# Writing a weight stream out in full on SyncE and GpSimd, in a kernel bound by TensorE

## The reference

```python
for l in range(DEPTH):                      # first_block
    h = x @ w_in[l]
    ...                                     # four attention groups -> mix
    y = _group_rmsnorm(mix, mix_g[l]) @ w_o[l]
    x = _layernorm(ALPHA * x + y, ln1_g[l], ln1_b[l])
    f = (jax.nn.silu(x @ w_gate[l]) * (x @ w_up[l])) @ w_down[l]
    x = _layernorm(ALPHA * x + f, ln2_g[l], ln2_b[l])
for l in range(DEPTH):                      # second_block
    h = x + 0.5 * swiglu(rms_norm(x, ffn1_norm[l]), ffn1_gate[l], ffn1_up[l], ffn1_down[l])
    z = rms_norm(h, mix_norm[l]) @ w_in[l]
    ...                                     # attention, convolution, RG-LRU
    h = h + jnp.concatenate([y_da, y_sc, y_lru], axis=-1) @ w_out[l]
    x = h + 0.5 * swiglu(rms_norm(h, ffn2_norm[l]), ffn2_gate[l], ffn2_up[l], ffn2_down[l])
return rms_norm(x, final_norm)
```

## Time and profile before

| what | value |
| --- | --- |
| median of 3 runs | 3143.33 us (3143.02 to 3143.93) |
| span of the profiled execution | 3141.2 us |
| time of the profiled execution beyond its span | not given; the median is 2.1 us above the span |
| busy share PE, POOL, DVE, ACT | 99%, 72%, 37%, 23% |
| mean granted TensorE clock | 0.998 |

### The profile page before, as it was taken

How to read it: one execution, slowest core, us unless ns; L and a number is a source line. 1 busy time by engine, 2 the same in 40 slices (tenths; PEclk the granted TensorE clock), 3 DMA queues, 4 the chain that set the end, 5 groups by cost and what they waited for, 6 DMA issues and landing times.

```text
span 3141.2 us, 44673 instructions
## 1 busy us (share of the span) xinstructions
PE 3116.4 (99%) x15518; PEld 2588.2 (82%) x15518; DVE 1147.4 (37%) x1874; ACT 713.8 (23%) x1474; POOL 2259.0 (72%) x3079
## 2 busy tenths in 40 slices
PE   8999999999999999999999999999999999999999
PEld 7879888898798888888887788888888887788887
DVE  5575111275751112632226542212222136542211
ACT  4453110054531100411112321110211022321100
POOL 5347877673468776788777398887888777398884
PEclk9999999999999999999999999999999999999999
DMA  5112322231123222232232132223222232132222
GB/s 185 48 41 86 109 93 95 93 108 42 47 88 104 96 95 90 84 102 98 95 112 92 41 101 95 98 95 100 94 94 100 94 111 88 41 108 94 100 94 68
DMA packets 83017, 284.07 MB, mean 90 GB/s; under 512 B 9531, under 2 KB 15068, under 8 KB 82652
## 3 DMA queue, kind: packets, MB, share of 16 engines
q1 hardware_dynamic: 77484, 273.70, 26.2%
q10 hardware_dynamic: 5424, 8.79, 0.8%
HBM read 278.79 MB, written 3.67 MB: 90 GB/s over the span
## 4 chain that ended last, share of the span: by engine, by line
PE 97%; DVE 2%; ACT 1%; issue 0%; DMA 0%; DVEq 0%; ACTq 0%
PE bank_v L537 21%; PE bank_v L539 20%; PE bank_v L538 20%; PE bank_a L537 9%; PE bank_a L539 9%; PE bank_a L538 9%; PE bank_v L881 1%; PE bank_a L860 1%; PE bank_s L1021 1%; PE bank_s L899 1%; PE bank_v L1036 1%; PE bank_s L591 0%; PE bank_s L1024 0%; PE bank_a L584 0%; PE bank_s L889 0%; PE bank_s L907 0%
## 5 line engine op out<-in xcount | busy, mean ns | idle before, releaser
L511 POOL TENSOR_TENSOR w_lo<-raw,w_hi 128x512 fp32r<-128x512 f32 x1024 | 1414.7, 1382 | 81.8
L508 POOL TENSOR_TENSOR zero<-zero 128x1 f32<-128x1 f32 x1024 | 277.3, 271 | 769.0 <-PE bank_v L539 578.8
L537 PE MATMUL bank_v<-xn_hi,w_hi 128*128 128x512 f32 (+1 forms) x1680 | 640.9, 381 | 8.1 <-DVE xn_lo L1700 8.0
L509 POOL CAST w_hi<-raw 128x512 fp32r<-128x512 f32 x1024 | 639.1, 624 | 0.0
L539 PE MATMUL bank_v<-xn_hi,w_lo 128*128 128x512 f32 (+1 forms) x1680 | 635.0, 378 | 0.0
L538 PE MATMUL bank_v<-xn_lo,w_hi 128*128 128x512 f32 (+1 forms) x1680 | 634.6, 378 | 0.0
L537 PE MATMUL bank_a<-xn_hi,w_hi 128*128 128x512 f32 (+1 forms) x1232 | 469.0, 381 | 2.3 <-ACT work L1248 1.4
L539 PE MATMUL bank_a<-xn_hi,w_lo 128*128 128x512 f32 (+1 forms) x1232 | 466.7, 379 | 0.0
L538 PE MATMUL bank_a<-xn_lo,w_hi 128*128 128x512 f32 (+1 forms) x1232 | 466.6, 379 | 0.0
L537 PE MATMUL bank_v<-h_hi,w_hi 128*128 128x512 f32 (+1 forms) x1122 | 422.9, 377 | 0.0
L538 PE MATMUL bank_v<-h_lo,w_hi 128*128 128x512 f32 (+1 forms) x1122 | 422.4, 376 | 0.0
(11 more groups left out here) (357 smaller groups left out, 3114.5 us busy)
## 6 DMA issues: line engine op xcount, KB each, us to landing
raw<-in_w_stream SPq DMA_DIRECT2D x516, 512.0 KB, 3.3
rope<-in_rope ACTq DMA_DIRECT2D x2, 1024.0 KB, 5.7
da_v<-t_rows ACTq DMA_DIRECT2D x2, 1024.0 KB, 6.5
out<-resid SPq DMA_DIRECT2D x8, 256.0 KB, 2.3
t_rows<-t_row ACTq DMA_DIRECT2D x1, 1536.0 KB, 7.4
resid<-in_x ACTq DMA_DIRECT2D x5, 256.0 KB, 7.2
mla_v<-in_alibi ACTq DMA_DIRECT2D x2, 512.0 KB, 7.5
resid<-in_x SPq DMA_DIRECT2D x3, 256.0 KB, 9.4
```

What stands on the lines that cost most here:

```text
L508: pool.tensor_tensor(zero[:, 1:2], zero[:, 0:1], zero[:, 0:1], ALU.add)
L509: pool.tensor_copy(w_hi[:, u, cut], raw[:, u, cut]).then_inc(*hi_split.done(("unit", u, n)))
L511: ins = pool.tensor_tensor(w_lo[:, u, cut], raw[:, u, cut], w_hi[:, u, cut].bitcast(F32), ALU.subtract)
L537: pe.matmul(out, lhs_hi, rhs_hi, start=first, stop=False)
```

## The change

Both loops are written out in Python over n = 4 to 515: each of the 512 units gets its own instructions, in which the waits compare with constants and the DMA's address is constant. The one-column addition ahead of each half is left out. The order of the loads, casts and subtractions, and what each waits for, stays. The programs of TensorE, VectorE and ScalarE are untouched.

```diff
-            with loop(sp, "stream", UNITS // SLOTS - 1) as i:
-                for u in range(SLOTS):
-                    sp.wait_ge(*w_split.before(("unit", u)))
-                    sp.dma_start(raw[:, u, :], t["w_stream"][i + 1, u]
-                                 ).then_inc(*raw_in[u].done("unit", 16))
+            for n in range(SLOTS, UNITS):
+                u = n % SLOTS
+                sp.wait_ge(*w_split.before(("unit", n)))
+                sp.dma_start(raw[:, u, :], t["w_stream"][n // SLOTS, u]).then_inc(*raw_in[u].done(("unit", n), 16))
...
-            with loop(pool, "stream", UNITS // SLOTS - 1):
-                for u in range(SLOTS):
-                    pool.wait_ge(*raw_in[u].after("unit"))
-
-                    for n, (left, cut) in enumerate(((half_used, slice(0, UNIT // 2)), (w_used, slice(UNIT // 2, UNIT)))):
-                        pool.wait_ge(left.sem, w_split.before(("unit", u))[1])
-                        pool.tensor_tensor(zero[:, 1:2], zero[:, 0:1], zero[:, 0:1], ALU.add)
-                        pool.tensor_copy(w_hi[:, u, cut], raw[:, u, cut]).then_inc(*hi_split.done(("unit", u, n)))
-                        pool.wait_ge(*hi_split.after(("unit", u, n)))
-                        ins = pool.tensor_tensor(w_lo[:, u, cut], raw[:, u, cut], w_hi[:, u, cut].bitcast(F32), ALU.subtract)
-                    ins.then_inc(*w_split.done(("unit", u)))
+            for n in range(SLOTS, UNITS):
+                u = n % SLOTS
+                pool.wait_ge(*raw_in[u].after(("unit", n)))
+                for k, (left, cut) in enumerate(((half_used, slice(0, UNIT // 2)), (w_used, slice(UNIT // 2, UNIT)))):
+                    pool.wait_ge(left.sem, w_split.before(("unit", n))[1])
+                    pool.tensor_copy(w_hi[:, u, cut], raw[:, u, cut]).then_inc(*hi_split.done(("unit", n, k)))
+                    pool.wait_ge(*hi_split.after(("unit", n, k)))
+                    ins = pool.tensor_tensor(w_lo[:, u, cut], raw[:, u, cut], w_hi[:, u, cut].bitcast(F32), ALU.subtract)
+                ins.then_inc(*w_split.done(("unit", n)))
```

## The result

| | before | after |
| --- | --- | --- |
| median (range) | 3143.93 us, 9 runs (3143.02 to 3144.33) | 3152.17 us, 9 runs (3146.81 to 3152.7) |
| ratio of the means, 95% interval | | 1.0023 (1.0014 to 1.0033) |
| profiled execution: span, mean clock | 3141.2 us, 0.998 | 3147.0 us (its time 3148.76), 0.998 |

The changed kernel is slower, by some 8 us in the median, and it has come to spread over 6 us where the kernel before keeps within 1.3. Ten more executions of it had a median of 3149.36 us (3147.71 to 3154.67), so the cost is 6 to 8 us. The forecast of 3143.2 us in 3141.0 to 3146.5 was wrong.

A forecast was written before the change was run, and what follows sets the result against it. TensorE was taken to bound the kernel; additions, waits, SyncE and code each brought 0 and VectorE's shifts -0.1 us on 3141.2 us, which with the median's 2.1 us offset gave 3143.2 us, range 3141.0 to 3146.5 us.

The forecast's parts named there:

- What bounds the kernel: Whole span: TensorE, busy 3116.4 of 3141.2 us, sets the time; none of its waits names GpSimd or a load.
- The additions go: GpSimd, 1024 one-column additions: removing them saves 133 us of GpSimd's occupancy (bounds 0 and 277) and 0 on TensorE.
- the 4.7 us of waits on VectorE: TensorE's waits: up to 4.7 us end on VectorE and could shrink; rival put at 3141.0 us, chance 0.08.
- The terms of GpSimd: GpSimd's busy time falls 133 us to about 2126, the cast's mean rises towards 700 ns, idle time grows as much.
- the excess of 79.7 us: GpSimd's additions: their time above the median, spent held; said to pass to the cast and not be saved.
- the sign's 2090 to 2150: GpSimd (POOL): busy time in us that would show the forecast right.
- The 2230 us given for an unrelieved GpSimd: GpSimd: rival that the start-up of 0.13 us passes to the cast; busy some 2230 us, time 3143.3 us, chance 0.04.
- Register waits, SyncE, code length: GpSimd's and SyncE's streams: constant waits save 0 to 6 us of GpSimd, none of TensorE; SyncE and longer code 0.
- As many may go away as come: VectorE's steps ahead of waiting matmuls: argument against new collisions, that those gained and lost may balance.
- VectorE's late steps collide anew: VectorE ahead of waiting matmuls: earlier casts hold a step by 1.09 us; three net collisions give 3146.6 us, chance 0.07.
- The rival on late refills: First projections and halved norms: instruction fetches delay GpSimd's refills, 2.6 us a hit; 3146 to 3151 us, chance 0.05.
- The clock: TensorE: two half-clock stretches of about 3.4 us, full elsewhere; one more or fewer is worth 1.7 us, within the range.

The follow-up runs named there:

- the kernels with the shortest middle waits (6.1, 6.9 and 7.2 us): On the changed kernel: no subtraction at the edges, 3139.49 us; additions and halved subtractions at the edges, 3143.94 us; every subtraction halved, 3143.82 us.

## Why the prediction was wrong

*What bounds the kernel*: right as far as it went. TensorE is busy for 99% (3118.1 us, 1.7 more than before, where at most 1 was expected), and no wait of it ends on GpSimd, before or after.

*The additions go; "on TensorE it is worth 0, because no wait of TensorE is ended by GpSimd"*: this is the step that failed, and what covers it was taken to be GpSimd's own slack. The waits name the last releaser only. GpSimd reaches TensorE through VectorE: a subtraction that has the port makes VectorE's next two-input step 1.1 us longer, and in the halved norms and the attention VectorE's steps release matmuls with nothing to spare. The prediction had both halves, the stretched step of the earlier trace rows and the 4.7 us of waits on VectorE, but its sum gave them -0.1 us, and it gave new collisions a chance of 0.07. It never asked which engine comes first at the port, with and without the additions. At 270 us of the trace before, the distance of 0.10 us could have been read. In place of the 0 the runs show 4.4 us more of TensorE's waits, and a median 8.2 us longer; with the additions back it is 3142.57 us.

*The terms of GpSimd*: the fall of its busy time was put at 133 us and is 161. The cast's mean was to rise to 700 ns and rose to 658, and its waiting for TensorE grew to 935.8 us, where 850 to 900 were expected. Of the excess of 79.7 us, 34.7 came to the cast and 19.4 to the subtraction; and the rest is gone from GpSimd. That POOL's 2097.7 us lie within the sign's 2090 to 2150 is no proof of the terms. The 2230 us given for an unrelieved GpSimd follow from no row.

*Register waits, SyncE, code length*: right as far as can be measured. With the additions kept, all three together give a ratio of 0.9987 to 1.0005, and SyncE alone 0.9992 to 1.0010. The instruction traffic grew by 24 packets and 0.2 MB.

*"As many may go away as come"*: wrong. The collisions that came (9 held steps against 5, and three longer attention steps) outweigh those that went. In the norms they repeat, since the cycles of the two engines keep step. The rival "VectorE's late steps collide anew" named the mechanism and the price of 1.09 us, and its 3146.6 us for three net collisions is near the fastest executions. Its sign, middle waits above 12 us, came true too (12.4, though 2.7 of them end on ScalarE). It had a chance of 0.07 only. The rival on late refills fell: no run with the subtraction whole made TensorE wait more than 0.5 us for GpSimd.

*The clock*: 1.7 us for one stretch was right. "At full elsewhere" was not: the matmuls up to 12.6 us run at half the clock too. Taking the clock as a noise of one stretch to either side was wrong. The changed kernel has the time of up to six stretches. They go with some 3.4 of the 8.2 us of the median's excess, and with nearly all of its spread. Why it has more of them isn't shown. It has waits of about a microsecond at more places, and the stretch at 642 us came in three traces, each with three held steps in a row just ahead of it. But the kernels with the shortest middle waits (6.1, 6.9 and 7.2 us) also have executions at a mean clock of 0.997, 3, 4 and 3 of 11, which the kernel before never has. No run made a gap by itself.

## What to carry to other kernels

An engine that ends nobody's wait can still sit on the critical path through a port that it shares: before a short, seemingly useless instruction is taken out of a neighbour's stream, look in the timeline at who starts first, by how much, and how long the loser is held. Where the lead is a tenth of a microsecond and the hold over one, shorten the hold (two halves of each subtraction won back all of it; with additions besides they gave nothing more) rather than trust the phase. And when a tile is added for an experiment, put it behind all others, or the placement is measured with it.

## What the runs showed of the hardware

Moving nearly all tiles by 320 bytes a partition made the 512-column matmuls start 228.6 ns apart instead of 226.2 (200 us over 875 and 884 of them), with clock, GpSimd and DMA as before, and the kernel 23 us slower. In that trace the high-by-high matmul is often followed after 231 or 232 ns, where it was 226 or 227; which of the tiles must lie how was not tried.
